# Two 32x512 units of the conditioning sum on TensorE, each placed one query piece later in the attention layer

## What is computed

```python
sh1, sc1, g1, sh2, sc2, g2 = [m[:, None, :] for m in jnp.split(silu_c @ ada_w[i] + ada_b[i], 6, axis=-1)]
h = _modulate(_rmsnorm_2(x, norm_w[i, 0]), sh1, sc1)
...
q, k, v = jnp.split(h @ w_qkv, [nq, nq + nk], axis=-1)          # 8 query heads, 2 key/value heads of 128
q = _rmsnorm_2(q.reshape(b, s, ATTN_HEADS, ATTN_HEAD_DIM), q_gain)   # per head, then rotary embedding
...
p = softmax(q k^T * ATTN_HEAD_DIM ** -0.5);  o = p v;  y_lat = o @ w_o
x = x + g1 * y
x = x + g2 * _conv_ffn(_modulate(_rmsnorm_2(x, norm_w[i, 1]), sh2, sc2), ...)
```

## Time and profile before

| | us |
|---|---|
| median of 3 executions | 1675.83 |
| lowest and highest | 1675.46 and 1678.76 |
| the profiled execution, its own time | 1690.07 |
| its span, first to last instruction | 1688.2 |
| PE busy | 1483.8 (88%) |
| DVE busy | 1105.5 (65%) |
| ACT busy | 583.5 (35%) |
| POOL busy | 828.1 (49%) |
| mean granted TensorE clock, as a share of 2.4 GHz | 0.945 |

### The profile page before, as it was taken

One profiled execution on the slowest core, in us unless ns is written; L12 is line 12 of the kernel. 1 busy time (PEld: TensorE's weight loads), 2 busy tenths in 40 slices (PEclk: granted clock), 3 DMA queues, 4 the chain that ended last, 5 costly groups with the idle time before them and its releaser, 6 DMA issues.

```text
span 1688.2 us, 22193 instructions
## 1 busy us (share of the span) xinstructions
PE 1483.8 (88%) x8310; PEld 1058.9 (63%) x8310; DVE 1105.5 (65%) x2162; ACT 583.5 (35%) x847; POOL 828.1 (49%) x746
## 2 busy tenths in 40 slices
PE   8999999756666799998878875889999989999999
PEld 7997675744222366665433431438998876699987
DVE  5865633797587868786756664317886547568865
ACT  6753331211121221232000001127665454466652
POOL 0025220467777765656667767642775113027750
PEclk9999999988787799999999987999999999999999
DMA  7447860698999999999999989995555554545451
GB/s 278 150 150 317 311 233 25 256 380 307 402 406 368 378 389 402 403 404 402 399 406 405 396 322 405 383 363 190 177 175 191 182 198 201 207 143 181 173 197 50
DMA packets 154251, 477.15 MB, mean 283 GB/s; under 512 B 10016, under 2 KB 12320, under 8 KB 150944
## 3 DMA queue, kind: packets, MB, share of 16 engines
q0 software_dynamic: 73728, 268.47, 41.1%
q1 hardware_dynamic: 80416, 207.27, 33.7%
HBM read 474.65 MB, written 1.05 MB: 282 GB/s over the span
## 4 chain that ended last, share of the span: by engine, by line
PE 56%; DVE 11%; DMA 11%; POOL 9%; issue 6%; ACT 2%; another core or an unknown queue 1%; ACTq 0%; DVEq 0%; POOLq 0%
PE ps L673 55%; POOL arena L2802 8%; DMA arena<-in_peer_v,cl 6%; DMA arena<-in_peer_u,arena 3%; DVE arena L1851 3%; PE ps L677 1%; POOL wring L2802 1%; DVE arena L1466 1%; DVE arena L1472 1%; DVE wring L1851 1%; DMA wring<-in_peer_u,arena 1%; DMA wring<-in_ada 1%; DVE st L2096 0%; DVE arena L1469 0%
## 5 line engine op out<-in xcount | busy, mean ns | idle before, releaser
L673 PE MATMUL ps<-arena,wring 128*128 128x256 f32 (+2 forms) x2360 | 603.4, 493 | 115.0 <-DMA arena<-in_peer_v,cl 92.2
L673 PEld LDWEIGHTS ps<-arena,wring 128*128 128x128 f32 (+1 forms) x2360 | 330.6, 167 | 368.6 <-issue 171.5
L1851 DVE CUSTOM_DVE_ANT_0 arena<-arena 128x1024 f32<-128x1024 f32 x214 | 257.2, 1225 | 141.4 <-DMA arena<-in_peer_u,arena 88.9
L2802 POOL DMA_INDIRECT arena<-in_peer_u,arena x214 | 243.0, 1136 | 201.7 <-DVE arena L1809 77.5
L2802 POOL DMA_INDIRECT arena<-in_peer_v,cl x214 | 231.0, 1080 | 85.5 <-issue 60.7
L673 PE MATMUL ps<-hhl,wh 128*128 128x256 f32 (+1 forms) x1056 | 252.4, 322 | 1.2 <-POOL hhl L2812 0.7
L2190 ACT ACT_TABLE_LOAD x64 | 82.1, 1283 | 406.5 <-DVE arena L1851 228.3
L1466 DVE TENSOR_TENSOR wl<-wring,wh 128x2048 fp32r<-128x2048 f32 (+1 forms) x76 | 168.1, 2212 | 60.0 <-ACT wh L2193 58.1
L673 PE MATMUL ps<-hhl,wl 128*128 128x256 f32 x704 | 198.5, 282 | 0.0
L673 PEld LDWEIGHTS ps<-hhl,wh 128*128 128x128 f32 x1056 | 175.6, 190 | 19.6 <-POOL hhl L2812 2.5
L2193 ACT ACTIVATE wh<-wring 128x2048 fp32r<-128x2048 f32 (+1 forms) x78 | 146.2, 1874 | 70.8 <-PE ps L673 69.0
(11 more groups left out here) (257 smaller groups left out, 2025.3 us busy)
## 6 DMA issues: line engine op xcount, KB each, us to landing
wring<-in_ups SPq DMA_DIRECT2D x33, 2048.0 KB
wring<-in_ada SPq DMA_DIRECT2D x24, 2048.0 KB, 11.5
wring<-in_ffn_w_down SPq DMA_DIRECT2D x12, 2048.0 KB
wring<-in_w_in SPq DMA_DIRECT2D x8, 2048.0 KB
wring<-in_ffn_w_down SPq DMA_DIRECT2D x6, 1536.0 KB
wring<-in_peer_wq SPq DMA_DIRECT2D x4, 2048.0 KB
wring<-in_attn_w_qkv SPq DMA_DIRECT2D x4, 2048.0 KB
wring<-in_w_out SPq DMA_DIRECT2D x2, 2048.0 KB
```

The source lines that it names most:

```text
L673: return pe.matmul(o, l, r, start=start, stop=stop)
L1851: ve.tensor_tensor_reduce(out=o, in0=o, in1=h2[:, t, :], scale=1.0, scalar=0.0, op0=MUL, op1=ADD, accum_out=dots[j % 2][:, k:k + 1]).then_ ...
L2802: po.indirect_dma_start(out=ring[n % NR], out_offset=None, in_=table, in_offset=bass.IndirectOffsetOnAxis(ap=which, axis=0)).then_inc(S[f" ...
```

## The change

The code differs in two lines of the list on PE:

```diff
         for g in (hn[0], hn[1], cond,
                   qp[0], qp[0], hn[0], hn[1], cond,
-                  qp[1], qp[1], hn[0], hn[1], hn[2], cond,
+                  qp[1], qp[1], hn[0], hn[1], hn[2],
                   qp[2], hn[2], hn[3],
                   qp[2], cond, hn[2], hn[3],
-                  qp[3], hn[3], hn[4],
+                  qp[3], hn[3], hn[4], cond,
                   qp[3], hs[0], hn[5], hn[4], hs[1], hn[5], hn[4], cond, cond, hn[5]):
```

## The result

The changed kernel takes 1670.13 us (median of 6, 1667.79 to 1671.99), the kernel before, run with it, 1676.53 us (median of 6). The ratio is 0.9956, 95% interval 0.9946 to 0.9966: faster by 6.4 us by the medians. Forecast were 1668.9 us, 0.41% and 6.9 us.

What follows compares the result with a forecast made beforehand. PE was taken to bound most of the kernel, its chain running through the `in_ada` 17 transfer. Wait 5.01 plus clock 0.86 and 0.88 gave 6.75, or 6.99 by start times; taking 6.9, 1675.83 - 6.9 = 1668.9 us, range 1666.8 to 1672.8.

Steps and rivals of the forecast that it cites:

- The place and the size of the wait: Ahead of the third unit, behind head norm 2's first step: PE's 5.01 us wait for transfer `in_ada` 17 goes.
- The clock: Behind that wait: without the fall to 1.2 GHz, the third unit saves 0.86 us, piece 2's first half 0.88.
- The ends given for this term: Gain 5.0 us if the clock doesn't fall in other executions, 9.05 if it stays at half through the first half-piece.
- Third unit at its new place: Behind piece 2's second half: no wait, PE there at 1392.0, the transfer landing at 1389.8, 2.2 us sooner.
- Fourth unit: Behind head norm 4's first step: costs nothing, freeing load 20's slot 2.7 us before load 19 goes out.
- POOL and DVE: Before the head loop: POOL's work moves up 7.9 us, PE's scores of head 0 6.9, and scores come last.
- The partial gain: Rival, from 1406 us on: DVE's sum or POOL's splits come out badly, only part arrives, 1671.5 us; chance 0.09.
- A new wait: Rival, at the seventh unit: load 19 late, PE waits 4.4 us, clock falls, no change, 1675.1 us; chance 0.07.
- Slower by the clock: Rival, in the head stage: narrow products and turns let the clock stay at 1.2 GHz, 1684 us; chance 0.03.
- The total: Whole kernel: 6.9 us off the median 1675.83, giving 1668.9 us, 0.41% faster; chance 0.81.

Runs made afterwards that it cites:

- the filled wait: Kernel before, plus 23 unused 128x128 products between the first step of head norm 2 and the third unit; 1685.67 us, ratio 0.9981 to the kernel before.
- only fourth moved: Kernel before with the fourth unit moved behind a step of head norm 4, the third left at its old place; 1689.72 us, ratio 0.9999.
- The half-way place: Changed kernel with the third unit half a query piece earlier, behind the first half of piece 2; 1684.16 us, ratio 0.9979 to the kernel before.

## Why the prediction was right

- **The place and the size of the wait.** Predicted 5.01 gone and none new: measured so, with 5.24 as the share of the wait in D. The prediction's own count from start to start was 6.99 - 1.74 = 5.25.
- **The clock.** Predicted 0.86 + 0.88 = 1.74; the filled wait gives 1.74 in D and 1.80 in the products themselves. The ends given for this term, 0 and 3.9, were wider than anything seen: the one other profile with the full wait (only fourth moved) has the unit at 1.86 us again, and the half behind it at 3.84 instead of 3.91. The Trainium skill ("TensorE: Matmul & The Clock Gate", Part 1) says that the number of slow products varies between runs with the gate's phase; two records don't test that, they differ by 0.07 us.
- **Third unit at its new place.** The transfer was to be 2.2 us ahead. The half-way place waited 2.09 us where 2.1 was reckoned, with the landing 6.00 us behind the norm step; the unit of the change starts 8.04 us behind it, so the transfer is 2.0 us ahead.
- **Fourth unit.** Predicted free of cost, with 2.7 us of cover. The unit ends at 1385.1, POOL's remainder at 1387.65, which is 2.6. No one waited for number 20, even with the unit 9.4 us later. That its place costs 0.3 us of PE's own time, by standing alone, was not seen. It is no part of the difference to the kernel before, where both units stood alone as well; start to start, the 1.00 us put on both places held.
- **POOL and DVE.** Loads 19 and 20 predicted 7.9 us sooner, measured 8.1; the scores of head 0 6.9, measured 26.01 - 19.12 = 6.89; PE's scores and not DVE last, as DVE's 0.77 us of idle time shows.
- **The partial gain.** Out: the gain at the scores, 6.89, is 6.98 at the dense stretch.
- **A new wait.** Out: number 19 was 8.1 us sooner, PE waited for no transfer in the head loop.
- **Slower by the clock.** Out for this order, 1.00 in the whole head stage. The Trainium skill's statement ("TensorE: Matmul & The Clock Gate", Part 4) that transposes do not count as activity for the clock in the same way is not borne out as a danger here: turned and narrow products, mixed with others, ran on at 1.00 in the 50.0 us of the head stage.
- **The total.** 6.9 predicted; 6.98 at the dense stretch, 6.4 and 6.8 by the medians. The forecast of 1668.9 took the median of three runs as its base, 1675.83, and six gave 1676.53; that is 0.7 of the 1.2 us by which it missed. The two durations of the last dense stretch were not foreseen: should the longer one belong to the change, the gain is 5.8 and not 6.9, still inside the forecast, and the agreement of the total would be partly luck.

## What to carry to other kernels

When a chain of waits runs through a transfer, find the instruction on the waiting engine that doesn't need it, and put as much of it ahead as the wait is long: here 7.3 us of work went ahead of a wait of 5.0. Count the clock with the wait, at the duration of the same instructions elsewhere in the trace, and don't take it that a short rest of the wait costs only itself: in the one profile of it, 2.1 us of wait were followed by 1.6 us of PE time lost to the clock, 0.9 of which reached the end of the stage. For a change of 0.4%, compare distances between two instructions in the profiles and not spans.

## What had not been expected of the hardware

The clock fell about 1.3 us after a wait of 2.09 us had ended, with PE busy, and PE lost 1.58 us by it, nearly the 1.80 behind the wait of 5.0. In the long wait 2.8 of its 5.0 us were already at the low clock, while PE was idle (a mean of 0.72); in the short case all of the low clock fell on work. Nine products without use took this fall away, in one profile. Each place at which the 32-column units stand apart costs PE 0.32 to 0.33 us against standing together. The last dense stretch has two durations, 61.27 us and 62.43 to 62.45, at the same granted clock.
